# Two more places for expert weights, and an earlier first filling of four, in a two-layer decoder kernel

## The reference

```python
h = h + jnp.dot(jnp.concatenate([o_nsa, o_conv, o_hgrn], axis=-1), w_out[l])   # token mixing
h = h + cross_attention(rmsnorm(h, norm_cross[l]), rmsnorm(mem, norm_mem[l]), ...)
h = h + hier_moe(rmsnorm(h, norm_ffn[l]), ..., expert_w_gate_up[l], expert_w_down[l])
```

## Time and profile before

| | |
|---|---|
| median of 3 runs (lowest, highest) | 1369.73 us (1364.55, 1371.67) |
| span of the profiled execution | 1364.9 us |
| TensorE busy, weight loads | 1218.5 us (89%), 723.8 us (53%) |
| VectorE, ScalarE, GpSimd busy | 483.4, 246.2, 77.5 us |
| bytes moved | 455.27 MB, mean 334 GB/s |

### The profile page before, as it was taken

How to read it: one execution, slowest core, us unless ns; L and a number is a source line. 1 busy time by engine, 2 the same in 40 slices (tenths; PEclk the granted TensorE clock), 3 DMA queues, 4 the chain that set the end, 5 groups by cost and what they waited for, 6 DMA issues and landing times.

```text
span 1364.9 us, 26014 instructions
## 1 busy us (share of the span) xinstructions
PE 1218.5 (89%) x10656; PEld 723.8 (53%) x10656; DVE 483.4 (35%) x1094; ACT 246.2 (18%) x573; POOL 77.5 (6%) x104
## 2 busy tenths in 40 slices
PE   7999997998898888898899999979999899898995
PEld 6978665444443444444488885644434444444442
DVE  4276326332322223222252663362222223222323
ACT  3022223111111111111120222221111111111111
POOL 0221200000000000000031230000000000000000
PEclk9999898999999999999999999979999999899998
DMA  8331348899999999999944113789999999999993
GB/s 360 114 140 62 124 183 372 338 427 429 430 428 427 429 430 429 427 428 429 416 181 151 52 63 124 312 341 428 429 427 428 429 429 428 428 428 429 429 427 158
DMA packets 33267, 455.27 MB, mean 334 GB/s; under 512 B 3776, under 2 KB 4160, under 8 KB 5312
## 3 DMA queue, kind: packets, MB, share of 16 engines
q1 hardware_dynamic: 33216, 454.59, 79.4%
HBM read 453.53 MB, written 1.05 MB: 333 GB/s over the span
## 4 chain that ended last, share of the span: by engine, by line
PE 63%; DMA 27%; DVE 4%; ACT 2%; issue 2%; SPq 1%; DVEq 0%; ACTq 0%
PE bank L515 60%; DMA share<-in_w_dn 24%; DMA streams<-in_w_gu 3%; DVE rest L1882 1%; PE bank L745 1%; SPq L391 1%; PE bank L574 1%; ACT rest L1290 1%; DMA share<-in_mem 0%; PE bank L1041 0%; DVE small L1588 0%; DVE h L1504 0%; ACT streams L1197 0%; ACT ring L1197 0%; ACT rest L1197 0%
## 5 line engine op out<-in xcount | busy, mean ns | idle before, releaser
L515 PE MATMUL bank<-share,rest 128*32 128x512 f32 (+1 forms) x2432 | 272.4, 528 | 51.9 <-DMA share<-in_w_dn 36.9
L515 PE MATMUL bank<-dense,rest 128*32 128x256 f32 (+2 forms) x1824 | 188.9, 476 | 8.4 <-DMA share<-in_w_gu 4.5
L515 PE MATMUL bank<-ring,rest 128*32 128x256 f32 (+1 forms) x1792 | 176.8, 482 | 3.3 <-DVE rest L1833 1.8
L515 PEld LDWEIGHTS bank<-share,rest 128*32 128x32 f32 x2432 | 99.1, 113 | 150.2 <-issue 119.1
L515 PE MATMUL bank<-streams,dense 128*128 128x256 f32 (+2 forms) x928 | 152.9, 339 | 1.8 <-ACT streams L1128 1.8
L515 PE MATMUL bank<-rest 96*128 96x512 f32 (+1 forms) x288 | 122.0, 579 | 34.2 <-DVE rest L1882 34.2
L515 PEld LDWEIGHTS bank<-rest,xhat 128*128 128x128 f32 x1056 | 126.1, 196 | 42.7 <-issue 42.7
L515 PEld LDWEIGHTS bank<-streams,dense 128*128 128x128 f32 (+1 forms) x928 | 132.9, 177 | 17.8 <-issue 3.5
L515 PE MATMUL bank<-rest,xhat 128*128 128x96 f32 x1056 | 137.0, 284 | 2.6 <-DVE rest L1791 2.6
L515 PEld LDWEIGHTS bank<-dense,rest 128*32 128x32 f32 (+1 forms) x1824 | 68.6, 111 | 116.6 <-issue 87.0
L515 PEld LDWEIGHTS bank<-ring,rest 128*32 128x32 f32 x1792 | 62.9, 111 | 106.8 <-issue 83.0
(11 more groups left out here) (238 smaller groups left out, 988.7 us busy)
## 6 DMA issues: line engine op xcount, KB each, us to landing
share<-in_w_dn SPq DMA_DIRECT2D x64, 2048.0 KB, 18.7
ring<-in_w_gu SPq DMA_DIRECT2D x48, 2048.0 KB, 20.8
dense<-in_w_gu SPq DMA_DIRECT2D x48, 2048.0 KB, 23.7
share<-in_w_gu SPq DMA_DIRECT2D x24, 2048.0 KB, 22.0
dense<-in_w_units SPq DMA_DIRECT2D x18, 2048.0 KB, 9.4
streams<-in_w_gu SPq DMA_DIRECT2D x8, 2048.0 KB, 26.9
dense<-in_w_units SPq DMA_DIRECT2D x4, 1024.0 KB, 5.9
dense<-in_w_units SPq DMA_DIRECT2D x2, 1184.0 KB, 5.6
```

The costliest lines, as they stand in the source:

```text
L515: return pe.matmul(out_ap, lhsT=lhsT, rhs=rhs, start=start, stop=stop, skip_group_check=True)
```

## The change

The descriptor scratch is set to 1 KiB. In what this frees lies a new buffer `spare` of one place. It becomes place 3 of odd pairs in both layers; in the last layer `streams` becomes place 4 of odd pairs. So there are 10 places in the first layer and 11 in the last. The refill of place 3 (`other_rows`) is now always for pair t+1; the refill of place 4 gets a function of its own (`large_down`), which in the last layer stands at the end of a turn and asks for pair t+1. The first layer takes over the last layer's table of leads. The place `spare` is first filled between unit 8 and unit 9. Places 1, 3, 4 and 5 of pair 0 are asked for once PE has filled "hot" (it turns the recurrence's output, so the recurrence's buffers are free), and no longer after "wo3"; place 2 of pair 0 and places 0 and 1 of pair 1 after "wo3".

```diff
-LEADS = [[3] * 4 + [2] * 4 + [1] * 4, [4] * 3 + [3] * 3 + [2] * 3 + [1] * 3]
+LEADS = [4] * 3 + [3] * 3 + [2] * 3 + [1] * 3
...
+        spare = sb("spare", [P, 4096])
...
         def odd_slot(s):
-            return dense[:, s, :] if s < 3 else eslot(s)
+            return dense[:, s, :] if s < 3 else spare[:, :] if s == 3 else eslot(s)
...
-            return streams[:, :, :].rearrange("p s c -> p (s c)") if s == 3 else odd_slot(s)
+            return streams[:, :, :].rearrange("p s c -> p (s c)") if s == 4 else odd_slot(s)
...
-            return s < 3 or l == DEPTH - 1 and s == 3
+            return s < 4 or l == DEPTH - 1 and s == 4
...
-                for u in range(3, 12):
+                for u in range(3, 9):
                     load_unit(u)
+                load_of(3, 3, True)
+                for u in range(9, 12):
+                    load_unit(u)
+                bank_full(sp, l, "hot")
+                alone(sp)
+                for s in (1, 3, 4, 5):
+                    load_of(s % 2, s)
                 bank_full(sp, l, "wo3")
                 alone(sp)
-                for s in range(1, 6):
-                    load_of(s % 2, s)
+                load_of(0, 2)
+                load_of(2, 0, True)
+                load_of(3, 1, True)
                 bank_full(sp, l, "memv")
                 alone(sp)
                 load_of(0, 0)
-
-                load_of(2, 0, True)
-                load_of(3, 1, True)
...
-                ahead = int(odd_apart(l, 3))
+                ahead = int(odd_apart(l, 4))
...
-                    load_of(3, 3, True)
+                    load_of(2, 4, True)
...
-                    load_expert((t + ahead) % PAIRS, 3, odd != (ahead == 1))
+                    load_expert((t + 1) % PAIRS, 3, not odd)
+
+                def large_down(t, odd, it):
+
+                    sp.wait_ge(efilled[5], it * 2 - 1)
+                    alone(sp)
+                    load_expert((t + ahead) % PAIRS, 4, odd != (ahead == 1))
...
                     load_expert(t % PAIRS, 5, odd)
-                    sp.wait_ge(efilled[5], it * 2 - 1)
-                    alone(sp)
-                    load_expert(t % PAIRS, 4, odd)
+                    if not ahead:
+                        large_down(t, odd, it)
...
                     if lead == 3:
                         down(t, odd, it)
-                    if ahead:
-                        other_rows(t, odd, it)
+                    other_rows(t, odd, it)
                     if lead == 4:
                         down(t, odd, it)
+                    if ahead:
+                        large_down(t, odd, it)
...
-    nc = _bacc.Bacc("TRN2", target_bir_lowering=False, num_devices=1)
+    nc = _bacc.Bacc("TRN2", target_bir_lowering=False, num_devices=1, dynamic_dma_scratch_size=1024)
```

More of the change, by code:

```diff
@@ L268, in hymba @@
         eloaded_of = [[sem(f"expert{s}_loaded_{l}") for s in range(6)] for l in range(DEPTH)]
-        odd_loaded_of = [[sem(f"odd_expert{s}_loaded_{l}") for s in range(3 + l)] for l in range(DEPTH)]
+        odd_loaded_of = [[sem(f"odd_expert{s}_loaded_{l}") for s in range(4 + int(l == DEPTH - 1))]
+                         for l in range(DEPTH)]
         vloaded = sem("memory_value_weights_loaded")
@@ L456, in down @@
                     load_expert(t % PAIRS, 5, odd)
-                    sp.wait_ge(efilled[5], it * 2 - 1)
-                    alone(sp)
-                    load_expert(t % PAIRS, 4, odd)
+                    if not ahead:
+                        large_down(t, odd, it)
                 def turn(t, odd, it, lead):
                     if lead == 0:
-                        if not ahead:
-                            other_rows(t, odd, it)
                         down(t, odd, it)
@@ L468, in turn @@
                     if lead == 1:
-                        if not ahead:
-                            other_rows(t, odd, it)
                         down(t, odd, it)
                     large_rows(t, odd, it)
-                    if lead >= 2 and not ahead:
-                        other_rows(t, odd, it)
                     if lead == 2:
@@ L479, in turn @@
                         down(t, odd, it)
-                    if ahead:
-                        other_rows(t, odd, it)
+                    other_rows(t, odd, it)
                     if lead == 4:
                         down(t, odd, it)
+                    if ahead:
+                        large_down(t, odd, it)
                 for t in range(1, 1 + STEPS_AHEAD):
-                    turn(t, t % 2 == 1, t, LEADS[l][t - 1])
+                    turn(t, t % 2 == 1, t, LEADS[t - 1])
                 odd_reg = sp.alloc_register(f"sp_odd_pair_{l}")
@@ L495, in _ @@
                 it = sp.snap(odd_reg, min_val=1, max_val=MAXP * PAIRS)
-                if not ahead:
-                    other_rows(PAIRS - 1, True, it)
                 down(PAIRS - 1, True, it)
```

## The result

The changed kernel takes 1363.04 us (median of 7 runs, 1359.87 to 1363.42), the kernel before, beside it on the same chip, 1369.73 us (7 runs, 1364.55 to 1373.12). The ratio is 0.9945 [0.9926, 0.9963]: 6.7 us faster, inside the range, 3.1 us above the forecast. The two profiled executions are only 3.9 us apart, 1361.0 against 1364.9 us.

What follows compares the result with a forecast made beforehand. Expert stages were taken as bound by their weight transfers (DMA share 1.00), not TensorE. One refill fewer per layer, - 4.92 us twice, other terms 0, gave 1355.1 us profiled, 1359.9 us on the median; range 1354 to 1367 us.

Steps and rivals of the forecast that it cites:

- Refills: Expert stages: one refill fewer in each layer, - 4.92 us twice, - 9.8 us, with start event and closing PE work unchanged.
- The sum: Whole kernel: profiled execution 1364.9 - 9.8 = 1355.1 us; the same difference on the median of 1369.73 gives 1359.9 us.
- rival 2: Start of refills: freed time given back by a shifted start, - 2.7 to + 3.3 us a layer; no change, 1369.7; chance 0.06.
- `spare`: Its first load, between units 8 and 9 of each layer: 4.92 us hidden in 24.20 us of idle transfers, cost 0.
- The four early loads: Mixing stage, from "hot" on: loads come 22.4 us earlier, nothing ends earlier, no contention with PE, ACT or DVE; 0.
- The scratch: Descriptor scratch: GpSimd issues no DMA and the loads use the hardware queue that SP feeds, so shrinking it costs 0.
- The leads: Refill order, first layer taking the last layer's table: transfers can't be busier than 1.00, no load held back; 0.
- What would show it: Signs in the new profile: 86 and 85 refills, share 1.00, last down weights 4.9 and 9.8 us earlier, stated transfer restart times.
- signs of being wrong: Share under 1.00 in first turns, a first refill that moves, longer instructions between 166 and 189 us, or unit 9 later.
- 1: Rival: one layer gives nothing because the first layer's end overlaps the next layer's units; - 4.9, 1364.8 us; chance 0.08.
- 3: Rival: the queue runs dry in the first six turns of a layer; slower, + 10.6 (1380.3 us) to + 41 us; chance 0.05.
- 4: Rival: PE's last 80 matmuls (9.02 us) and start escape the clock drop; - 3 to - 5 more, about 1355 us; chance 0.04.

Runs made afterwards that it cites:

- f_before: The kernel before, with 3 and 5 matmuls that nobody reads filling two TensorE waits of each layer's mixing stage; 1361.84 us, ratio 0.9952.
- f_after: The changed kernel, with 3 and 5 matmuls that nobody reads filling two TensorE waits of each layer's mixing stage; 1351.80 us, ratio 0.9878.
- late4: The changed kernel with the four early loads (places 1, 3, 4, 5 of pair 0) back behind "wo3"; 1360.80 us, ratio 0.9929.
- again: The changed kernel measured once more, unedited, in another job; 1362.35 us, ratio 0.9948.
- f_late4: f_after with the four early loads back behind "wo3"; 1351.35 us, ratio 0.9875.
- scratch: The kernel before with a descriptor scratch of 1 KiB and nothing in the freed room; 1371.40 us, ratio 1.0018.

## Why the prediction was right, and where it failed

**Refills: right.** - 4.92 twice; measured - 4.66 and - 4.93 in the profiled pair, - 4.96 and - 4.98 between f_before and f_after. That the stage is as long as its refills holds: share 1.00 and 425 GB/s throughout.

**The sum: the step that failed.** The sum took the start of both stretches as fixed, and rival 2 allowed a shift by the clock but said "what PE does before is not changed, so I see no reason for a shift". The work is unchanged, and still the starts moved by + 1.79 and + 4.91 us in the profiled pair, to 1361.0 against the 1355.1 of the sum. Rival 2 also looked in the wrong place: it priced the 8.80 us ahead of the first refill, where the clock is low in both kernels, and not the wait for ScalarE some 90 us earlier, where it can be either. (Its own sum is off as well: two shifts of 3.3 us and a lost place come to 1371.4, not 1369.7, still no change.) By the line above the difference at equal clock is 9.2, on the medians 6.7; so the size of the refill term was right, and what is missing on the medians is, as far as these runs show, that of a clock that the two kernels didn't share. That 1363.04 lies inside the range is due to the range's width, not to the sum.

**Around the span.** "Next to nothing lies around it" is wrong: the profiled run of the changed kernel is timed at 1363.04 us with a span of 1361.0, so 2.0 lie around it. The difference between kernels isn't touched by that.

**Costs put at 0.** `spare`: hidden, the transfers idle from 92.2 to 112.3 us after it; unit 9 was issued at 111.49 instead of 110.77, at a clock of 0.91 instead of 0.96 between 60 and 100 us. In late4 and again, with `spare` and a clock of 0.96, unit 9 follows unit 8 after 28.1 us, as before. The four early loads: nothing, by f_late4. No contention: the 128x512 addition beside them (169 to 213 us, by form) takes what it took in the earlier trace rows, and 128x512 matmuls up to 188.6 us take 592 ns on average in both kernels:

```profile
L1510 DVE TENSOR_TENSOR h<-h,bank 128x512 f32<-128x512 f32 x4 | 2.7, 686 | 17.3 <-PE bank L521 17.3
```

The scratch: nothing that these runs can tell. The leads: 0 in the total, but not in the parts. With the old leads a place in the first layer would have shortened the refills by 431.62 - 428.44 = 3.2 us, and the new table gives the other 1.8. "The transfers can't be busier than 1.00, so nothing is gained" overlooked that with ten places the old table would have been under 1.00.

**What would show it.** Refill counts, shares, 2 MB between units 8 and 9 and the early 8 MB came as said. Three signs did not: transfers resumed at 247.2, not within 1 us of 245.20; in the last layer at 919.7, 2.1 us behind the 917.60 of before and not 4.9 ahead; and the last down weights landed 2.9 us earlier in both layers (672.87 for 675.75, 1340.41 for 1343.32), not 4.9 and 9.8. All three are the two shifts: 1.79, 6.7 - 4.66 = 2.0, and 1.79 - 4.66 and 6.7 - 9.6 = -2.9. Of the signs of being wrong, two came: the first refill moved, and unit 9 came 0.7 us later, though in late4 and again `spare` costs it nothing.

**Rivals.** 1: no, both layers give. 3: no idle transfers in the first turns; the shortest landings are 8.9 and 8.4 us, above the 4.92. 4: a small part, the tail's 0.97 us, as the last 9.02 us of PE lie off the chain now. 2: in part, by the clock.

Open: whether the changed kernel's clock is lower by 1.6 thousandths of itself or by chance of 14 runs (the difference is 2.3 times its standard error), whether it is the change that brings the last layer's fall after the wait for ScalarE (three profiles with it, two without), and what decides after equal waits.

## What to carry to other kernels

When a stage is bound by its transfers and every buffer is refilled through one queue, one more buffer is worth one transfer per pass, and no engine needs to get faster for it; but the order of refills has to keep the queue busy (with the old leads 3.2 us of the 4.96). Such a gain of 0.7% is as large as what the clock of a waiting TensorE takes or leaves: compare profiled pairs stage by stage, and look at the granted clock of a stage before explaining its change by the edit. Useless products in PE's waits can be worth more than the edit, if they end before the wait does.

## What was not expected of the hardware

- The same 3.04 us of waiting was followed by no low clock in one kernel (1.00) and by some 10 us of 1.2 GHz in another (0.82), with the same instructions around it, and the latter also without the early loads (late4). In the first layer it was so within one program, 0.87 in before and 1.00 in scratch. The Trainium skill ("TensorE: Matmul & The Clock Gate", section "Part 1: The HAM clock gate (the "warmup" mystery)") says that the chip judges TensorE's activity on a rhythm of its own that doesn't start with the kernel. That would fit these rows; no run here set that rhythm, so it isn't shown.
- Eight fillers a layer, 7.3 us of useless work, took the kernel before to 0.9952 of its time and the changed one from 0.9948 to 0.9878 in the same job; eleven took it to 0.9865. Sixteen took before to 1.0021.
